# A prompt convolution of 31 taps, shared between GpSimd and VectorE

## The reference

```python
for l in range(DEPTH):                       # DEPTH = 2
    x = x + 0.5 * swiglu_ffn(rmsnorm(x, ...), ...)
    cols = rmsnorm(x, P['mix_norm'][l]) @ P['w_in'][l]
    glu = cols_a[..., :CONV_CH] * jax.nn.sigmoid(cols_a[..., CONV_CH:])
    u = jnp.concatenate([hist, glu], axis=1)         # 30 zero rows ahead of the prompt
    y_a = conv_module(u, P['conv_w'][l], ...)        # depthwise, CONV_WIDTH = 31 taps, 256 channels
    y_b = combine_dilations(parts)                   # dilated attention, three groups
    y_c, S = rwkv_time_mix(cols_c, ...)              # a recurrence over the tokens
    x = x + jnp.concatenate([y_a, y_b, y_c], axis=-1) @ P['w_out'][l]
    x = x + cross_attend(rmsnorm(x, ...), mk, mv, ...)
    x = x + 0.5 * swiglu_ffn(rmsnorm(x, ...), ...)
```

## Time and profile before

| what | value |
| --- | --- |
| median of 3 runs | 1688.08 us (1686.42 to 1690.28) |
| the profiled execution | 1688.16 us, its span 1686.4 us |
| TensorE busy | 1600.4 us, 95% of the span |
| VectorE busy | 1072.8 us, 64% |
| ScalarE busy | 753.5 us, 45% |
| GpSimd busy | 295.1 us, 17% |
| line 543, products on GpSimd | 120 instructions, 1205 ns each on average |
| line 559, sums on GpSimd | 60 instructions, 1450 ns each |
| line 1910, low parts of units on VectorE | 386 instructions, 1265 ns each |

### The profile page before, as it was taken

How to read it: one execution, slowest core, us unless ns; L and a number is a source line. 1 busy time by engine, 2 the same in 40 slices (tenths; PEclk the granted TensorE clock), 3 DMA queues, 4 the chain that set the end, 5 groups by cost and what they waited for, 6 DMA issues and landing times.

```text
span 1686.4 us, 32180 instructions
## 1 busy us (share of the span) xinstructions
PE 1600.4 (95%) x13716; PEld 1513.2 (90%) x13716; DVE 1072.8 (64%) x1613; ACT 753.5 (45%) x1293; POOL 295.1 (17%) x256
## 2 busy tenths in 40 slices
PE   8999999899799999999999999998988998999997
PEld 7999998886698879999999999988867896999997
DVE  6776468866653457775477754788675643777744
ACT  5444358324544445443354433573254433544433
POOL 1000008991010010000010000199700000100000
PEclk9999999897999999999999999999979999999999
DMA  6766744303546764544445667442234477644541
GB/s 235 270 244 249 287 156 135 110 3 84 185 159 257 292 243 161 172 164 164 160 159 216 237 253 270 132 149 71 42 115 180 148 278 300 218 164 162 174 161 45
DMA packets 39967, 303.72 MB, mean 180 GB/s; under 512 B 4817, under 2 KB 4977, under 8 KB 7409
## 3 DMA queue, kind: packets, MB, share of 16 engines
q1 hardware_dynamic: 37488, 288.92, 47.4%
q0 software_dynamic: 2048, 11.17, 2.4%
q10 hardware_dynamic: 288, 1.57, 0.3%
HBM read 291.88 MB, written 36.83 MB: 195 GB/s over the span
## 4 chain that ended last, share of the span: by engine, by line
PE 78%; DVE 12%; ACT 4%; DMA 3%; issue 1%; SPq 0%; DVEq 0%; ACTq 0%
PE bank L675 22%; PE bank L677 21%; PE bank L676 21%; DVE w_lo L1910 3%; PE bank L859 3%; DMA slots<-stream 3%; ACT w_hi L1384 1%; PE bank L1284 1%; PE bank L1269 1%; ACT arena L1384 1%; DVE h_mem L1926 1%; PE bank L1338 1%; PE bank L823 1%; PE bank L1157 1%; PE bank L1139 1%
## 5 line engine op out<-in xcount | busy, mean ns | idle before, releaser
L1910 DVE TENSOR_TENSOR w_lo<-slots,w_hi 128x1024 fp32r<-128x1024 f32 x386 | 487.0, 1265 | 340.6 <-ACT w_hi L1384 336.5
L675 PE MATMUL bank<-h_hi,w_hi 128*128 128x288 f32 x1936 | 580.4, 300 | 20.5 <-DVE w_lo L1910 11.4
L676 PE MATMUL bank<-h_lo,w_hi 128*128 128x288 f32 x1936 | 573.7, 296 | 0.0
L677 PE MATMUL bank<-h_hi,w_lo 128*128 128x288 f32 x1936 | 571.8, 295 | 0.0
L1384 ACT CAST w_hi<-slots 128x1024 fp32r<-128x1024 f32 x390 | 406.3, 1046 | 290.1 <-PE bank L677 258.6
L675 PEld LDWEIGHTS bank<-h_hi,w_hi 128*128 128x128 f32 x1936 | 365.4, 189 | 29.5 <-DVE w_lo L1910 10.9
L677 PEld LDWEIGHTS bank<-h_hi,w_lo 128*128 128x128 f32 x1936 | 367.1, 190 | 0.0
L676 PEld LDWEIGHTS bank<-h_lo,w_hi 128*128 128x128 f32 x1936 | 366.2, 189 | 0.3
L515 POOL TENSOR_TENSOR arena<-arena 128x288 f32<-128x288 f32 x45 | 46.2, 1027 | 971.8 <-ACT arena L1434 969.5
L677 PE MATMUL bank<-hid_hi,w_lo 128*128 128x288 f32 x704 | 207.7, 295 | 0.0
L675 PE MATMUL bank<-hid_hi,w_hi 128*128 128x288 f32 x704 | 207.2, 294 | 0.5 <-DVE w_lo L1910 0.5
(11 more groups left out here) (331 smaller groups left out, 2112.1 us busy)
## 6 DMA issues: line engine op xcount, KB each, us to landing
slots<-stream SPq DMA_DIRECT2D x237, 1024.0 KB, 5.0
out_win3k<-win3k SPq DMA_DIRECT2D x2, 4080.0 KB
out_win3v<-win3v SPq DMA_DIRECT2D x2, 4080.0 KB
h_mem<-stream SPq DMA_DIRECT2D x4, 1024.0 KB, 10.7
out_win2k<-win2k SPq DMA_DIRECT2D x2, 2032.0 KB
out_win2v<-win2v SPq DMA_DIRECT2D x2, 2032.0 KB
con<-consts SPq DMA_DIRECT2D x1, 2340.0 KB, 10.8
arena<-mem_in POOLq DMA_DIRECT2D x2, 1024.0 KB, 5.6
```

The costliest lines, as they stand in the source:

```text
L675: mm(out, lhs[0], rhs[0], start=start, stop=False)
L676: mm(out, lhs[0], rhs[1], start=False, stop=False)
L677: return mm(out, lhs[1], rhs[0], start=False, stop=stop)
L1910: D(tt(out, src, hi.bitcast(F32), ALU.subtract), name)
```

## The change

Of the 31 taps, GpSimd keeps taps 0 to 19 and VectorE takes taps 20 to 30. GpSimd starts behind `kk_rec` instead of behind the gated unit. VectorE's taps are summed in `late_taps`, in place of the first two of `h`'s tiles, which nothing reads there; tap 20 is a TENSOR_SCALAR for each channel tile, and each later one a SCALAR_TENSOR_TENSOR that multiplies and adds. They stand in four places of VectorE's list: two ahead of `state(0)`, two ahead of the ropes, two ahead of `state(1)` and five ahead of `s_x`. A last sum adds `late_taps` to GpSimd's `ycv`, under the name `conv_p`, and the readers wait for that.

```diff
+POOL_TAPS = 20
...
+        late_taps = h[:, 0:2, 0:TP]
...
-                pool.wait_ge(vector_done, VL.value(l, ("glu", 1)))
-                pool.wait_ge(tensor_done, TL.value(l, ("in", "cols", RAW - 1)))
+                pool.wait_ge(vector_done, VL.value(l, "kk_rec"))
...
-                for tap in range(1, TAPS):
-                    if tap + 1 < TAPS:
+                for tap in range(1, POOL_TAPS):
+                    if tap + 1 < POOL_TAPS:
...
-                        pe.wait_ge(pool_done, PL.value(l, ("summed", TAPS - 1)))
+                        pe.wait_ge(vector_done, VL.value(l, "conv_p"))
...
-                act.wait_ge(pool_done, PL.value(l, ("summed", TAPS - 1)))
+                act.wait_ge(vector_done, VL.value(l, "conv_p"))
...
+                def taps(first, stop):
+                    for tap in range(first, stop):
+                        settle()
+                        for ch in range(2):
+                            src = up[:, ch, tap:tap + TP]
+                            if tap == POOL_TAPS:
+                                D(ts(late_taps[:, ch], src, pr("conv_w", ch * TAPS + tap), None, ALU.mult))
+                            else:
+                                D(stt(late_taps[:, ch], src, pr("conv_w", ch * TAPS + tap), late_taps[:, ch], ALU.mult, ALU.add))
...
                 pair(1, 2, (2, 3))
+                taps(POOL_TAPS, POOL_TAPS + 2)
                 state(0)
                 pair(1, 3, (2, 3))
                 pair(1, 4, (0, 1))
+                taps(POOL_TAPS + 2, POOL_TAPS + 4)
                 for i6 in range(2 * G):
                     rope(i6)
+                taps(POOL_TAPS + 4, POOL_TAPS + 6)
                 state(1)
...
+                taps(POOL_TAPS + 6, TAPS)
+                settle()
+                dve.wait_ge(pool_done, PL.value(l, ("summed", POOL_TAPS - 1)))
+                D(tt(ycv[:, :, 0:TP], ycv[:, :, 0:TP], late_taps, ALU.add), "conv_p")
```

## The result

The changed kernel took 1671.95 us (median of 4 runs, 1670.62 to 1672.79) against 1688.49 us of the kernel before on the same chip (4 runs, 1686.42 to 1690.28). The ratio is 0.9903, 95% interval 0.9887 to 0.992. The profiled execution took 1671.88 us, with a span of 1670.1 us. One run in this study, the profiled one of e9 further down (1758.32 us), had a mean granted clock of 0.84 instead of 0.98, and no comparison uses it.

The account below looks back on a forecast made before the run. The prediction took the chain led by TensorE (78% of the span), without GpSimd, as the bound. A gain of 5.1 us in each layer, 2 x 5.1 = 10.2 us off 1688.16 us, gave 1678.0 us, range 1674 to 1684.

Parts of the forecast that it names:

- Part 1: Input projection: GpSimd starting behind the reciprocal removes TensorE's 2.33 us wait and the low clock; gain 5.1 us a layer.
- the clock stays low: Rival for tile 17: TensorE's clock stays low even without the wait; gain 2.4 us a layer, 1683.3 us; chance 0.08.
- Then VectorE becomes the last: Projection's end: VectorE, with 17.4 us of work from the keys, ends at 314.6 and decides over TensorE's 313.6.
- would bound the gain at some 6: Projection: if all GpSimd disturbance of VectorE's 17.4 us fell out, TensorE would limit the gain to some 6 us.
- More disturbance: Rival in the projection: two more GpSimd meetings in VectorE's 17.4 us leave 3 us a layer, 1682 us; chance 0.10.
- Part 2: GpSimd's convolution: with twenty taps started at 292.9 it ends at 364 instead of 377.3.
- Part 3: VectorE's eleven taps in the recurrence: 0.91 us a tap, mostly hidden in pauses; 0.1 us taken for the ropes.
- that is the first place alone: Taps: GpSimd still runs only beside those ahead of `state(0)`; a meeting would leave 0.1 us of 2.68 uncovered.
- GpSimd wasn't the reason: Rival: VectorE's long instructions come from elsewhere, the reciprocal stays at 295.77 and nothing moves, 1688 us; chance 0.06.
- Slower: Rival ahead of the ropes: late GpSimd delays them 2 us, TensorE's clock falls, 7 us lost against 5.1; 1692; chance 0.04.

Follow-up runs that it names:

- e9: Changed kernel with VectorE's first two taps moved into pauses of the recurrence's last levels and later taps one place up: 1672.65 us, ratio 0.9923 to the kernel before.
- e5: Changed kernel with three extra memsets on VectorE ahead of the key norms, delaying the reciprocal by 4.0 us: 1686.2 us, ratio 1.0011 to the kernel before.
- e6: Changed kernel with two extra memsets on VectorE ahead of the key norms, delaying the reciprocal by 2.7 us: 1685.93 us, ratio 1.0004 to the kernel before.
- e4: Changed kernel with GpSimd's taps 1 to 19 left out and VectorE's taps kept: 1670.92 us, ratio 0.9919 to the kernel before.
- before_again: The kernel before, unaltered, run and profiled once more against itself: 1683.41 us, ratio 0.9999.
- e7: Changed kernel with GpSimd starting behind VectorE's keys, at 297.89 instead of 292.15: 1678.9 us, ratio 0.9957 to the kernel before.
- e1: Changed kernel with GpSimd's start put back behind the gated unit, taps still split: 1681.38 us, ratio 0.9968 to the kernel before.

## Why the prediction was wrong, point by point

**The sign and the main place were right, and the size was too small.** The profiled pair differs by 16.3 us, and 10.2 were forecast. The 6.1 between them are 2.3 + 1.8 - 0.6 + 1.9 + 0.7, in the order of the points below.

**Part 1, up to tile 17: right.** The reciprocal came 2.9 us earlier within the stretch (34.73 to 31.85; 2.9 forecast). The idle ahead of L799 is gone, the clock is 1.00, and ScalarE's copy of tile 17 comes 303.31 - 296.87 = 6.44 us earlier. The token shift had already come 0.86 us earlier, so 5.6 remain, the forecast's number. The keys start at 296.35, for 297.2 - 0.86 = 296.3 forecast. That the wait brings the clock down was an assumption then; e5 and e6 show it (in e5 the clock is at 0.50 before L799 begins), and the rival *the clock stays low* falls.

**Part 1, "Then VectorE becomes the last": the step that failed.** I kept VectorE's 17.4 us from the keys to the last low part "as it is", disturbance included. It measured 311.15 + 1.21 - 296.35 = 16.0 us. GpSimd's meetings with it had moved: L2095 took 1.05 instead of 2.15, L2101 1.25 instead of 2.15, and one low part 2.31 instead of 1.21; that is 0.9 of the 1.4 us, and the rest is spread over several instructions. So VectorE was done at 312.4, in time for the last tile, and TensorE ran through: its copies are 3.20 us apart to the end, where before had 3.91. The projection gained 5.6 + 0.7 = 6.3 us at its last copy, (323.22 - 316.07) - 0.86, instead of 5.1. Over both layers that is 12.5 instead of 10.2: the 2.3. The text had this bound ("would bound the gain at some 6") and chose the other engine. The choice rested on meetings whose number in 17 us can't be read from one profile; it was worth 1.4 us of slack against a deficit of 1.0 (314.6 against 313.6). e4 shows the bound directly. *More disturbance* reached the time in none of the 12 layers in which GpSimd worked there (28.93 to 28.95 us to the first level).

**Part 2: GpSimd's end at 366.5 instead of 364**, 2.5 us late, or 3.4 with the earlier token shift. The four products behind the first two took 6.12 us where 4.6 were assumed; before had already taken 5.50 for the same four, a row that the forecast didn't use. That is 1.5 of the lateness. I put it down to a VectorE without pauses there, which no run isolates. In layer 0 it did no harm. In layer 1 it did, as the next point shows.

**Part 3: right in layer 0, wrong in layer 1.** Where no operation met GpSimd the taps measured 0.89 to 0.91 us each, and the last ten operations took 4.55 for 4.6. In layer 0 the first rope started 0.04 us behind its matmul, as forecast. In layer 1 it started 1.06 us behind it, in all three profiles. More than 0.5 us was the prediction's own sign that this part is wrong. The step that failed is "that is the first place alone". GpSimd's lateness (part 2) reached the second place: it ended at 1187.07 + 2.89 = 1189.96, and the taps began at 1188.34. One tap operation took 1.50 us instead of 0.48, where 0.1 was taken for the ropes. The Trainium skill's rule on the shared port (SBUF — State Buffer, "SBUF: two separate sides") lets a VectorE operation with two SBUF inputs, as a tap is, and a GpSimd instruction that reads SBUF lock each other out. The trace agrees: the 1.0 us was lost once, in one of the four. At the first place L2217 took 1.10 and 0.95 us beside GpSimd for the 0.61 of e4, and the pair behind it in layer 1 took 1.90 for 0.89; `state(0)` came 0.2 us late there. `s_x` came 0.2 to 0.3 us later behind the first rope, for 0.5 forecast; I had called this hidden, and it is the 0.6 above.

**What the sum left out.** The first: 1.8 us between first level and first rope in both layers together. The prediction had it only at the edge of the range, as 1 us for the whole kernel. It is 2.8 us gained ahead of the first tap (41.68 and 40.93 us in before, 40.95 and 38.87 in after) and 1.0 lost at the rope of layer 1. In that piece TensorE's clock was at its lower level for a time in both layers of before, and in layer 0 alone of after. In the 6 of the 24 profiled layers where it stayed up the piece took 38.9 to 39.2 us. With GpSimd silent (e4) it took 38.9 to 39.0 though the clock fell. So the clock and GpSimd both have a part in it; which of them gave the 2.8 us, and whether the change did, isn't shown. The second: 1.9 us ahead of the token shift. From the last row of layer 0's cross attention to the token shift of layer 1, the first profile of before took 459.94 us, before_again 459.14, and all three profiles of after 458.9. In layer 0 the token shift starts at 259.09 in that profile and between 257.8 and 258.7 in the eleven others. Nothing of the change stands there, and it is the slowest of the twelve at both places: this was luck. The third: 0.7 us behind `s_x`, which is luck too: the three profiles of after differ among themselves by up to 2.9 us in one layer there.

**The time that was compared.** The forecast took the profiled run of before for the kernel. It was a run with the long wait and the low clock in both layers, and the other profile of before has the low clock in one. Against the median of all runs of before the forecast of 10.2 would be 1676.4, which the changed kernel's 1672.8 still beats by 3.6 us.

**The other rivals.** *GpSimd wasn't the reason* falls by the table's first column: 31.85 us wherever it is silent and no memset stands there, 33.4 to 34.7 where it runs. *Slower* is real. Its first part stands in layer 1 of the changed kernel itself, at 1.06 us. In e7, with GpSimd's end 4 us later, the lateness was 1.95 for the 2 of the prediction, but the clock followed in layer 0 alone. From the first level to `s_x` it took back 4.4 to 5.1 us in layer 0 and 3.3 to 3.6 in layer 1, instead of 7.

## What to carry to other kernels

An engine off the critical path can cost the path time by slowing one short chain that TensorE waits for. Look for single instructions that take a microsecond more than their like, ask which engine works beside them, and move that work to where nobody waits. Then ask TensorE first what its own pace allows, since that bound is steady from run to run and the meetings aren't.

When a kernel's own runs spread by nearly 1% (15.3 us over 74 runs here, against 6.4 over the changed kernel's 15; the standard deviations are 3.9 and 1.5), take several profiles before pricing anything. One profile showed only one outcome of the lottery.

## What the runs showed of the hardware

- An idle of TensorE of 2.1 to 3.4 us ahead of L798 was followed by the 1.2 GHz level in 9 layers of 9, of before, before_again, e1, e5 and e6 alike; an idle of 0.96 us or none was not, in 15 of 15. How soon it came back after the same wait differed: from 300 to 303 the granted clock was 0.52 in the first profile and 0.89 in before_again. In the ropes of e7 an idle of 1.96 us was followed by the lower level in layer 0, and one of 1.97 us in layer 1 was not.
- A full meeting of VectorE and GpSimd costs VectorE 1.0 to 1.1 us once (0.24 to 1.28, 0.30 to 1.40, 0.48 to 1.50, 1.22 to 2.32 us); some instructions lost less (L2217: 0.61 to 0.95 or 1.10). Which instruction is hit changes between layers of one program (L2073: 0.29 or 1.40 us in before_again). L2171, which reads a PSUM bank, took 0.56 us with GpSimd beside it (after) and 0.56 without (e4).
- With GpSimd silent and the clock up, the two stretches of the projection repeat to 0.03 us over 14 layers and several chips.
